# More constant products in a two-layer diffusion step's mLSTM and router, and the mLSTM output spread over the attention steps

## What is computed

```python
def ab_mixer(w_in, w_out, q_norm, k_norm, gate_bias, out_norm, h, ctx=None):
    aq, ak, av, bq, bk, bv, bo, bg = jnp.split(h @ w_in, split_idx, axis=-1)
    ...
    a_out = blocked_attention(aq, jnp.concatenate([ctx_k, ak], axis=1),
                              jnp.concatenate([ctx_v, av], axis=1))
    hm, cT, nT, mT = mlstm_bidir(bq, bk, bv, gates, c0, n0, m0)
    b_out = rms_norm(hm, out_norm).astype(h.dtype) * jax.nn.sigmoid(bo.reshape(b, n, B_HEADS, B_HEAD_DIM))
    out = jnp.concatenate([a_out.reshape(b, n, A_WIDTH), b_out.reshape(b, n, B_WIDTH)], axis=-1) @ w_out
    ...

def hier_moe(x, wg, bg, we, be, w1, w3, w2):
    g_logits = (xt @ wg + bg).astype(jnp.float32)
    g_sel = jnp.argmax(g_logits, axis=-1)
    ...
    e_logits = (xt @ we + be).astype(jnp.float32).reshape(t, N_GROUPS, EXPERTS_PER_GROUP)
    ...
    rank = jnp.take_along_axis(jnp.cumsum(onehot, axis=0), eid[:, None], axis=1)[:, 0] - 1
    ...
        hid = jax.nn.silu(xi @ w1[e]) * (xi @ w3[e])
        return hid @ w2[e]
```

## Time and profile before

| | us |
|---|---|
| median of 3 runs | 1628.11 |
| lowest and highest of them | 1628.05, 1630.46 |
| the profiled execution, its own time | 1629.48 |
| its span, first to last instruction | 1627.7 |
| TensorE busy in the span | 1524.1 (94%) |
| VectorE busy in the span | 445.2 (27%) |
| mean granted clock of TensorE | 0.972 |

### The profile page before, as it was taken

The page is one execution under the profiler, slowest core; times in us unless marked ns, Lnnn a source line. Parts: engine busy times, 40 slices in busy tenths (PEclk is TensorE's granted clock), DMA queues, the critical chain, the costliest instruction groups (busy, mean ns, idle before and its releaser), DMA issues.

```text
span 1627.7 us, 21580 instructions
## 1 busy us (share of the span) xinstructions
PE 1524.1 (94%) x8459; PEld 720.2 (44%) x8459; DVE 445.2 (27%) x1055; ACT 299.2 (18%) x647; POOL 142.7 (9%) x194
## 2 busy tenths in 40 slices
PE   5999888989999999999979998898999999999991
PEld 3555785454333333333324555544333333333340
DVE  0012697333111111111123027634311111111114
ACT  3100236111111111111111006411111111111111
POOL 1002110101000000000005000100000000000000
PEclk9999999989999999999989999999999999999996
DMA  9898980268999999999969522204999999999983
GB/s 347 324 341 176 384 271 2 82 283 325 429 427 428 428 428 429 428 427 428 427 266 313 184 104 78 82 17 201 419 427 427 428 427 428 428 428 427 428 371 120
DMA packets 82919, 521.56 MB, mean 320 GB/s; under 512 B 10130, under 2 KB 11610, under 8 KB 56240
## 3 DMA queue, kind: packets, MB, share of 16 engines
q1 hardware_dynamic: 70400, 491.87, 74.1%
q0 software_dynamic: 12464, 28.93, 6.1%
HBM read 511.01 MB, written 20.22 MB: 326 GB/s over the span
## 4 chain that ended last, share of the span: by engine, by line
PE 87%; DVE 8%; DMA 2%; ACT 2%; issue 1%; POOL 0%; POOLq 0%; DVEq 0%; SPq 0%; ACTq 0%
PE psum L932 27%; PE psum L945 14%; PE psum L913 10%; PE psum L564 6%; PE psum L878 5%; PE psum L590 5%; PE psum L938 3%; PE psum L587 3%; PE psum L925 2%; PE psum L919 2%; PE psum L487 2%; PE psum L470 2%; PE psum L530 1%; PE psum L791 1%; DVE area_m L1398 1%
## 5 line engine op out<-in xcount | busy, mean ns | idle before, releaser
L932 PE MATMUL psum<-ring,area_t 128*64 128x512 f32 x1024 | 449.9, 592 | 1.8 <-issue 0.9
L933 PE MATMUL psum<-ring,area_t 128*64 128x512 f32 x1024 | 450.0, 592 | 0.0
L932 PEld LDWEIGHTS psum<-ring,area_t 128*64 128x64 f32 x1024 | 140.1, 137 | 291.9 <-issue 291.9
L945 PE MATMUL psum<-ring,area_t 128*64 128x512 f32 x1024 | 233.8, 598 | 2.2 <-DVE area_t L1907 2.2
L1878 DVE COPY area_q<-psum 64x512 f32<-64x512 f32 x64 | 44.5, 695 | 558.5 <-PE psum L933 558.4
L913 PE MATMUL psum<-area_h,area_t 128*64 128x512 f32 x768 | 175.9, 592 | 3.1 <-DVE area_t L1892 3.1
L933 PEld LDWEIGHTS psum<-ring,area_t 128*64 128x64 f32 x1024 | 140.1, 137 | 0.0
L2114 POOL DMA_INDIRECT pair_rows<-area_q,idx x64 | 62.4, 975 | 878.8 <-ACT area_q L1318 878.5
L945 PEld LDWEIGHTS psum<-ring,area_t 128*64 128x64 f32 x1024 | 68.5, 136 | 122.0 <-issue 122.0
L1308 ACT ACTIVATE area_q<-psum 64x512 f32<-64x512 f32 x64 | 37.8, 590 | 403.1 <-PE psum L933 403.1
L913 PEld LDWEIGHTS psum<-area_h,area_t 128*64 128x64 f32 x768 | 55.7, 137 | 111.1 <-issue 108.9
(11 more groups left out here) (267 smaller groups left out, 1409.4 us busy)
## 6 DMA issues: line engine op xcount, KB each, us to landing
ring<-in_moe_w SPq DMA_DIRECT2D x192, 2048.0 KB, 15.2
ring<-in_ada_w SPq DMA_DIRECT2D x24, 2048.0 KB, 19.9
ring<-in_na_w_in SPq DMA_DIRECT2D x6, 2048.0 KB, 18.7
ring<-in_ab_w_in SPq DMA_DIRECT2D x5, 2048.0 KB, 18.7
area_m<-mod_ready POOLq DMA_DIRECT2D x6, 1024.0 KB, 10.2
area_q<-pair_rows SPq DMA_DIRECT2D x6, 1024.0 KB, 6.9
ring<-in_ab_w_out SPq DMA_DIRECT2D x2, 2048.0 KB, 15.5
area_g<-mod_ready POOLq DMA_DIRECT2D x4, 1024.0 KB, 9.7
```

Source lines behind the costliest of these rows:

```text
L932: pe.matmul(banks[2 + u][0:64, :], lhsT, w1[:, k, :], start=(k == 0), stop=(k == KT - 1))
L933: mm = pe.matmul(banks[2 + u][64:128, :], lhsT, w3[:, k, :], start=(k == 0), stop=(k == KT - 1))
L945: mm = pe.matmul(banks[6 + u][64 * j:64 * j + 64, :], hidT[u][:, k, :], w2[:, k, 512 * j:512 * j + 512], start=(k == 0), stop=(k == 3))
```

## The change

It has three parts.

- In `mlstm`, TensorE gets two constant products between the modulation products and the wait for the gates' logarithms, two behind the sums and modulation products of stage 0, and one between the two directions' scores of stage 1.
- `mixer_b_out(t)` takes a second argument that names one of its three passes, and a table `BOUT_STEPS` tells in which attention step each pass runs: steps 6 to 12, one or two passes each.
- Behind the output projection TensorE waits for all mixed rows ahead of the logits of tiles 1 and 2, and gets a constant product there (for layer 1 only at tile 2); there is one more behind the logits of tile 1, and eight, not seven, ahead of `ranks`.

```diff
+        BOUT_STEPS = {6: ((0, "root"), (0, "gain")), 7: ((0, "gate"),), 8: ((1, "root"),),
+                      9: ((1, "gain"), (1, "gate")), 10: ((2, "root"),), 11: ((2, "gain"),),
+                      12: ((2, "gate"),)}
...
                 ada_step("turned")
+                idle_products(5, 2)
 
                 pe.wait_ge(S["lf_ready"], 1)
...
+                        if s == 1 and d == 1:
+                            idle_products(6, 1)
                         if s:
...
                         ada_step(("waited", s))
+                        if s == 0:
+                            idle_products(6, 2)
                         pe.wait_ge(S["combined"], v + 1)
...
+
+                    pe.wait_ge(S["x_mixed"], (l + 1) * NT * OUT_CHUNKS)
+                    idle_products(3, 1 if l == 0 or t == 2 else 0)
                     logits(l, t)
-                idle_products(3, 7)
+                    if t == 1:
+                        idle_products(3, 1)
+                idle_products(3, 8)
                 ranks(l)
...
-            def mixer_b_out(t):
-
-                if t == 0:
+            def mixer_b_out(t, factor):
+
+                if t == 0 and factor == "root":
                     v.wait_ge(S["hm_rooted"], 1)
                     do(v.reciprocal(hss[:, :, :], hss[:, :, :]))
...
-                tt(tmp1, out, last(hss[:, t, :], BD), ALU.mult)
-                tt(tmp1, tmp1, ogain, ALU.mult)
-                v.wait_ge(S["ogate_done"], t + 1)
-                tt(dst, tmp1, ab[:, t, BO:BO + 512].rearrange("p (u s) -> p u s", u=4), ALU.mult, "bout_ready")
+                if factor == "root":
+                    tt(tmp1, out, last(hss[:, t, :], BD), ALU.mult)
+                if factor == "gain":
+                    tt(tmp1, tmp1, ogain, ALU.mult)
+                if factor == "gate":
+                    v.wait_ge(S["ogate_done"], t + 1)
+                    tt(dst, tmp1, ab[:, t, BO:BO + 512].rearrange("p (u s) -> p u s", u=4), ALU.mult, "bout_ready")
...
-                    if l == 0 and 7 <= i < 7 + NT:
-                        mixer_b_out(i - 7)
+                    if l == 0:
+                        for t, factor in BOUT_STEPS.get(i, ()):
+                            mixer_b_out(t, factor)
```

## The result

| | before | changed |
|---|---|---|
| median, us | 1630.51 | 1623.51 |
| lowest, highest, us (8 runs each) | 1628.05, 1633.09 | 1619.53, 1629.40 |
| changed to before, ratio | | 0.9942 (0.9925 to 0.9960) |
| profiled execution's span, us | 1627.7 | 1618.1 |

The kernel is faster by 0.58% of 1630.5, which is 9.5 us by the ratio; the two medians differ by 7.0 us, and the ratio's interval, 6.5 to 12.2 us, holds both. 1623.5 lies inside the range of 1617.5 to 1625.5 and 2.2 above the forecast.

What follows compares the result with a forecast made beforehand. TensorE, holding 87% of the chain, was taken as the bound, at half clock in four stretches. Gains 0.9 + 0.6 + 1.4 + 3.0 + 2.3 = 8.2 us from 1629.48 gave 1621.3 us, range 1617.5 to 1625.5.

Steps and rivals of the forecast that it cites:

- Part 4: Last rows' turns to ranks: products hold the clock; 3.0 us in layer 0, 2.3 in layer 1; bounds -3.4, 5.3.
- Rival (b): Expert stage swallows the router's gain as first weights land late: 1624.3 us, or 1626.6 with layer 1; chance 0.12.
- (c): Router: clock falls ahead of the last logits despite the products, which then stand in the way: 1632.5 us; chance 0.04.
- Part 3: Attention: mLSTM output passes spread over steps 6 to 12; gain 1.4 us, bounds 0.4 and 1.7.
- The term of the two passes: Attention: seven passes, not nine, stand ahead of step 11's normalisation: 1.45 us less.
- The other one: Attention: VectorE's 0.28 us idling ahead of step 7's key copy is filled by work that comes earlier.
- rival (a): Short holes hold no clock: mLSTM's first products and attention give only their lower bounds: 1623.2 us; chance 0.24.
- Part 1: mLSTM, two products ahead of the cumulative sums: clock holds for the row products; 0.9 us, bounds 0 and 1.7.
- Part 2: mLSTM's second half, three products in two waits: third row products' wait goes; 0.6 us, bounds -0.4 and 0.6.
- five products' worth of work between the two holes: mLSTM's second half: real work between the two filled waits, with which the clock should hold.
- The single product: mLSTM: lies in the 1.39 us wait ending at 212.77; fits at full clock, ends 0.4 us late at low.
- the base: Whole kernel: the profiled execution's 1629.48 us, from which the summed gain was subtracted.

Runs made afterwards that it cites:

- twelve products: Changed kernel with twelve constant products ahead of the ranks instead of eight: ratio 0.9990 to the kernel before.
- without the pair: Changed kernel with the two constant products behind stage 0's sums in the mLSTM taken out: ratio 0.9921 to the kernel before.
- third profile of the changed kernel: Changed kernel unaltered, run again as the yardstick beside later kernels: median 1622.25 us, ratio 0.9936 to the kernel before.
- router only: Kernel before with only the constant products around the router's logits and ahead of the ranks: median 1625.25 us, ratio 0.9954.
- the product ahead of the first logits: Changed kernel minus the mLSTM pair, plus one constant product ahead of tile 0's logits in each layer: 1621.21 us, ratio 0.9924 to before.
- the same again: Second run of the changed kernel minus the mLSTM pair, plus a product ahead of tile 0's logits per layer: 1623.92 us, ratio 0.9944 to before.

## Why the prediction was right, and where it was off

**Part 4, the mechanism right, the size too small.** With the products the router takes 18.0 to 18.1 us in both layers, nine profiles out of nine (the twelve products apart). Without them, the four profiles have 21.05, 20.07, 24.00 and 23.97 in layer 0 (the clock of the last two fell again behind the ranks, 1.70 and 1.69 us more to the first expert's hidden products, which is counted here) and 20.27, 20.31, 20.07 and 21.76 in layer 1. Means 22.3 and 20.6, so 4.2 and 2.5 us, together 6.7, where I had 3.0 and 2.3. The steps held: the product between the turns and the last logits, these at 1.98 us, eight products of 7.11 (I had 6.9). Twelve products cost all of their 3.44 us, so whatever goes beyond eight is paid. What was mis-sized is the state before. I took one execution's fall (0.50 for 10.2 us in layer 0) for the kernel's; of the three others one fell for 6.8 us, two for 13.7 and again for 3.4. "The expert stage is as long as before" held too: from the first hidden products to layer 1's first product the changed kernel takes 490.6, against 490.1, and ranks to end 512.15, against 512.00. Rival (b) is out. So is (c): the logits' 36 columns did not let the clock fall in any of the nine.

**Part 3, right, and a little small.** The new order gives 37.40 us of attention in the three profiles in which the clock stays up, and 37.61 to 37.66 in the five in which it falls for 3.4 us (from 273.7 in the changed kernel, just behind the turn), against 39.41 to 39.81 with the old order (four): 2.0 in the mean of these eight, beyond my upper bound of 1.7. The term of the two passes came out as worked out (1.45). The other one was too small: the wait ahead of unit 7's turn is 1.70 to 1.71 and not 2.2, and counted from the first scores that turn comes 0.60 us sooner (24.66, before 25.26), where I had 0.28. Once, without the pair, the clock fell for longer:

```profile
270.70:277.50 6.80, 6.57 (x32) 4.24 (x32) 5.32 (x14) 3.41 (x12) 0.00 (x0) 0.50 0.00 0
```

Then the attention takes 39.08: 0.4 left, the lower bound that I gave, and the mean of all nine is a gain of 1.8. So rival (a)'s mechanism for this part exists; the full size of it came in one of nine.

**Part 1, in two of eight.** With the two products ahead of the cumulative sums, VectorE's first wait was 2.21 us in two profiles (without the pair, and twelve products) and 3.50 to 3.94 in the other six: mean 3.33, against 3.86 in the six without them, a gain of 0.5 for my 0.9. My value was the middle of two bounds, and both occur. Two of eight against none of six comes by chance in three cases of ten, so that the products did it isn't shown. Ahead of the row products stand nine products of 4 or 8 columns, eighteen matmul records; I had counted the records as products, here and in the words on the kernel. The time of about 3 us is as I read it.

**Part 2, the step that failed.** I wrote that the pair fits into the wait of 1.82 us, charged nothing for it, and took 0.6 us for what it brings. The wait is 1.8 us only if the clock stays up in TensorE's own work ahead of it. In seven of the fourteen profiles it falls there, that work takes 1.5 to 1.6 us more, and the pair stands in the way. Of the five profiles with the pair it lay in the wait in one; in the other four VectorE waited 0.91 to 1.06 us for the number products. The price of 0 was one execution's.

Part 1 may have a share in this, which isn't shown. The fall from 195.6 to 199.9 stands in six of the eight profiles with the two products ahead of the cumulative sums, the two in which they held the clock among them, and in one of the six without; and it stands in none of the five whose first fall was as long as before (6.8 us). If it is so, the parts can't be summed: what shortens the first fall brings the second, and takes the cover from the pair.

What the pair was to bring is small too. The third set of row products is waited for no more in the changed kernel, as I had said. But that wait, 0.39 to 0.61 us, is there in only four of the nine profiles without the pair, those with a first fall of 6.8 us, which fell again from 209.9 to 214.9. The third profile of the changed kernel had such a first fall, did not fall again and did not wait: one case in which the pair may have held the clock. (What I called five products' worth of work between the two holes is eight products of 128 columns, 1.9 us there.) In the mean the pair saves 0.2 us of that wait and adds 0.8 of the other. The single product fits in all eight profiles, with 0.7 to 1.2 us of waiting left behind it.

Later in the mLSTM the clock also falls near 225, behind the one-column products, and VectorE waits for the number products there by 1.10 to 2.74 us in seven of the fourteen profiles, three of which have no product of the mLSTM; the prediction didn't look there. In the one of 2.74 us TensorE also idled 2.3 us among the modulation products, waiting for nothing that the profile shows. These four waits of VectorE (the first and the third row products, the number products twice) are the whole difference: the mLSTM takes 61.1 to 61.2 us and their sum in twelve profiles, and 61.4 and 61.5 in the other two, before and router only.

The mLSTM's mean is 65.8 us with all five products, 65.6 without the pair and 66.3 with none: at most 0.7, from means of values that differ by 1 to 3 us. The times agree that it is nothing that can be measured (0.9998), where I had 1.5.

**The sum.** By stages the three parts bring 0.5 + 1.8 + 6.7 = 9.0 us; the ratios, 0.9942, 0.9939 and 0.9936, give 9.5 to 10.5. I had 8.2. That the median came out 2.2 above the forecast all the same has its reason in the base: I took the profiled execution, 1629.48, and let the shown median of 1628.11 stand beside it. The kernel before has medians of 1630.5 to 1633.8 in its four sets of runs, single ones from 1626.7 to 1638.2; over all 74, on several chips, the median is 1632.6, over the 20 of the changed kernel 1623.1. So the base was 3.1 us too low and the gain 1.3 too small, and the two partly cancel. That the forecast came within 2.2 us is luck to that extent, and so it is that part 4's surplus made up for what parts 1 and 2 lacked. The direction of the change is not luck, nor is the router as the place of most of the gain.

**What stays open.** Falls inside the output projections, where the change does nothing: layer 0 has them in seven of eleven profiles without the product ahead of the first logits, layer 1 in three of eleven, 1.7 or 3.4 us each; with it in none of three, which chance alone gives in one case of ten. By those means it would be worth 2.1 us, and the medians (1621.21, 1623.92, 1623.21 against 1622.82 and 1622.25) don't bear that out, so no version is shown to beat the changed one. And six of the ten profiles with the router's products have a fall in the last expert that the four without them have not. It costs 1.5 us, as TensorE's timeline of "the same again" shows: the down products of two experts, the second behind a wait of 1.12 us and partly at the low clock.

```profile
1567.74 3.65 PE L952 MATMUL psum<-ring,area_t 128*64 128x512 f32 x16
...
1580.95 5.35 PE L952 MATMUL psum<-ring,area_t 128*64 128x512 f32 x16 [1.12 <-DVE area_t L1923]
```

Nothing ties it to the router, six of ten against none of four can be chance, and it wasn't tried on its own. Nor was the added wait for the mixed rows: every kernel with the router's products has it.

## What to carry to other kernels

A constant product in a wait is free only as long as the wait is there. Ask how long the engine's own work ahead of it takes at the low clock too: here a fall of 3.4 us in that work left 0.2 of 1.8 us, and the products were in the path. Where the clock falls in other places in each execution, one profile gives neither the base nor a part's worth; compare the stage's length over several profiles, since the stages resolve 0.1 us where the medians of whole runs resolve 3. A row of constant products pays up to the point at which what follows is ready, and each one beyond it costs its full 0.86 us.

## What the runs showed of the hardware

- Turns of float32 data, without any product between them but the logits of 36 columns, held the granted clock at 1.00 over 14.6 us in layer 0 and 13.2 in layer 1, at the end 56 turns in a row over 6.3 us.
- The clock falls in other places in each execution of one program, and the same stage then costs nothing, 1.7 or 3.4 us more (the output projection of layer 0: 47.47, 49.16, 50.84). The same work of TensorE in the mLSTM, from stage 0's turned weights to the number products, takes 10.36 us, or 11.9 to 12.0 with a fall of 3.4 us in it.
- The clock fell near 225 us, behind products of one column and of 32 rows (L687, L490), in ten of fourteen profiles and not in the other four, the kernel before among these, though that part is the same in all of them.
- In the changed kernel it fell there in all three profiles, for 6.8, 6.8 and 3.4 us; VectorE had to wait in the first two only.
